# Moving the second mixer's preparation between the units of its weight stream, and rotating three tiles for normalised terms

## The reference

```
p = h @ w_in                                 # 1024 -> 2816 channels
ps, pc = p[:1792], p[1792:]                  # shifted part, convolution part
ps = ps + (token_shift(ps) - ps) * mu        # the frame before mixed in
r, k, v, xw, xa, xg = split(ps)              # 512, 512, 512, 64, 64, 128
decay = exp(-DECAY * sigmoid(w0 + tanh(xw) @ w_up))
a = sigmoid(a0 + xa @ a_up);   g = sigmoid(xg) @ g_up
kk = heads(k * k_k);  kk = kk * rsqrt(max(sum(kk*kk), 1e-12))   # 8 heads of 64
k = k * (1 + (a - 1) * k_a)
y = recurrence(r, decay, k, v, -kk, kk * a)  # 64 frames at a time
y = normalised per head * gn_w + gn_b + sum(r * k * r_k) * v
out_a = y * g
c = causal convolution of width 31 over glu(pc), one filter per channel
out_b = silu(layernorm(c))
return concatenate([out_a, out_b]) @ w_out
```

## Time and profile before

| what | value |
|---|---|
| median of three runs | 3702.67 us |
| the profiled execution's own time | 3696.74 us |
| its span in the profile | 3695.1 us, 45654 instructions |
| PE busy | 3479.5 us (94%) |
| DVE busy | 2001.3 us (54%) |
| ACT busy | 1122.0 us (30%) |
| mean granted TensorE clock | 0.976 of full |

### The profile page before, as it was taken

One profiled execution on the slowest core, in us unless ns is written; L12 is line 12 of the kernel. 1 busy time (PEld: TensorE's weight loads), 2 busy tenths in 40 slices (PEclk: granted clock), 3 DMA queues, 4 the chain that ended last, 5 costly groups with the idle time before them and its releaser, 6 DMA issues. The chain is left out here.

```text
span 3695.1 us, 45654 instructions
## 1 busy us (share of the span) xinstructions
PE 3479.5 (94%) x18472; PEld 2718.8 (74%) x18478; DVE 2001.3 (54%) x2662; ACT 1122.0 (30%) x1465; POOL 154.0 (4%) x128
## 2 busy tenths in 40 slices
PE   7999999999999999957799999999999989999998
PEld 6887776688878886837578886765788866568886
DVE  5667545522354334897753335696434348953334
ACT  2222335322232223232332223325322233452222
POOL 0000000000000000000000000330000012300000
PEclk8999999999999999979899999999999999999999
DMA  6554221122222222210012222210222221102221
GB/s 225 190 183 171 80 105 46 57 91 102 91 80 93 101 92 87 92 46 4 2 69 91 102 91 80 80 69 24 82 100 93 100 80 69 58 35 103 91 103 68
DMA packets 47213, 325.64 MB, mean 88 GB/s; under 512 B 5232, under 2 KB 5488, under 8 KB 8672
## 3 DMA queue, kind: packets, MB, share of 16 engines
q1 hardware_dynamic: 41792, 290.10, 22.0%
q0 software_dynamic: 5280, 33.52, 2.5%
HBM read 321.51 MB, written 2.10 MB: 88 GB/s over the span
## 5 line engine op out<-in xcount | busy, mean ns | idle before, releaser
L1991 PE MATMUL PS<-HH,WH 128*128 128x512 f32 x2264 | 895.2, 395 | 25.5 <-DVE HL L2392 18.9
L2374 DVE TENSOR_TENSOR WL<-RAW,WH 128x2048 fp32r<-128x2048 f32 x264 | 613.7, 2325 | 503.8 <-ACT WH L2227 498.2
L1992 PE MATMUL PS<-HL,WH 128*128 128x512 f32 x2264 | 884.8, 391 | 0.0
L1993 PE MATMUL PS<-HH,WL 128*128 128x512 f32 x2264 | 884.6, 391 | 0.0
L2227 ACT ACTIVATE WH<-RAW 128x2048 fp32r<-128x2048 f32 x264 | 503.1, 1906 | 330.2 <-PE PS L1993 322.1
L1991 PEld LDWEIGHTS PS<-HH,WH 128*128 128x128 f32 x2264 | 427.2, 189 | 140.6 <-issue 33.1
L1993 PEld LDWEIGHTS PS<-HH,WL 128*128 128x128 f32 x2264 | 427.0, 189 | 90.8
L1992 PEld LDWEIGHTS PS<-HL,WH 128*128 128x128 f32 x2264 | 427.3, 189 | 87.5 <-issue 1.2
L1991 PE MATMUL PS<-AH,WH 128*128 128x512 f32 x1056 | 412.3, 390 | 3.3 <-DVE A L2440 3.0
L1992 PE MATMUL PS<-AL,WH 128*128 128x512 f32 x1056 | 411.4, 390 | 0.0
L1993 PE MATMUL PS<-AH,WL 128*128 128x512 f32 x1056 | 411.3, 390 | 0.0
(11 more groups left out here) (395 smaller groups left out, 3668.2 us busy)
## 6 DMA issues: line engine op xcount, KB each, us to landing
RAW<-in_w SPq DMA_DIRECT2D x264, 1024.0 KB, 4.8
E<-in_ada POOLq DMA_DIRECT2D x28, 1024.0 KB, 5.0
E<-in_ada SPq DMA_DIRECT2D x4, 1024.0 KB, 11.8
G<-in_ada SPq DMA_DIRECT2D x4, 1024.0 KB, 19.3
X<-in_x SPq DMA_DIRECT2D x1, 2048.0 KB, 13.7
out_x<-A SPq DMA_DIRECT2D x8, 256.0 KB, 2.1
G<-in_cos POOLq DMA_DIRECT2D x4, 256.0 KB, 3.2
G<-in_sin POOLq DMA_DIRECT2D x4, 256.0 KB, 3.4
```

The lines of the kernel that those rows point to most:

```text
L1991: nc.tensor.matmul(out, wh, xh, start=start, stop=False)
L1992: nc.tensor.matmul(out, wh, xl, start=False, stop=False)
L1993: return nc.tensor.matmul(out, wl, xh, start=False, stop=stop)
L2374: nc.vector.tensor_tensor(WL[:, w % 2, :], RAW[:, w % 2, :], WH[:, w % 2, :].bitcast(F32), ALU.subtract).then_inc(w_lo, 1)
```

## The change

The order of the units becomes pc2, lora2, k2, r2, v2. The preparation is cut into pieces that stand between the units on all three engines. PE does the decay products behind unit 5, the rate products behind 6, the sum of squares of kk behind 7 (now to 32 rows a tile, all four tiles in one bank), the spreading of the root back to the heads behind 8, and the bonus behind 9. The projections use four banks in turn instead of eight, and the last unit its own two. The shift is made by ACT's copy with a scale (1 - mu) and one DVE operation that reads the bank. k_k, r_k and k_a are applied by ACT (r_k to the constant block matrix), and the bonus is copied out by ACT and multiplied by v later. The kk term takes the decay of the frame before out of the same sums, so that one exponential and one subtraction go. The last unit's shift, the multiplication of the bonus by v and the low half of the second w_out unit are done by DVE within the pairs. The taps run over up to three tiles in turn, so that a tap waits for the one before the last; 89 of the 124 stand in the stream and 35 in the pairs. The terms of normalised outputs take three tiles in turn and wait for the addition three tiles back.

```diff
-        "mix2": [("pc2", 4), ("r2", 2), ("k2", 2), ("v2", 2), ("lora2", 1)],
+        "mix2": [("pc2", 4), ("lora2", 1), ("k2", 2), ("r2", 2), ("v2", 2)],
...
+        B2, KK2 = A[:, 0:4, :], A[:, 4:8, :]
+        INV2, DEC2 = G[:, 16:20, :], A[:, 12:16, :]
+        TMP2 = [E[:, 15, :], E[:, 14, :], G[:, 20, :], G[:, 21, :]]
+        BV2 = [SG[:, 0, :], SG[:, 1, :], V[:], R0[:]]
+        RKB2 = A[:, 20, :]
+        BONUS_BANK, LAST_BANKS = (0, 1, 4, 5), (6, 7)
...
+        TAPS_IN = [9, 11, 11, 11, 9, 9, 14, 6, 2, 3, 4]
+        TAPS_LEVEL = [(2, 1, 2, 1, 1), (3, 2, 2, 1, 1), (3, 2, 2, 1, 1), (3, 2, 2, 1, 2)]
...
+        def chunk_of(q):
+            return (LO2, XG2)[q] if q < 2 else (K2, R2, V2)[(q - 2) // 4][:, (q - 2) % 4, :]
+        def mu_of(q):
+            return 12 + q if q < 2 else (4, 0, 8)[(q - 2) // 4] + (q - 2) % 4
+        def unit_banks(u):
+            return LAST_BANKS if u == U2 - 1 else (2 * (u % 2), 2 * (u % 2) + 1)
...
+            pool.dma_start(LEVELS[:, 0:7 * CH + 160], T["levels"]).then_inc(m2_loads, 16)
...
+                if 2 <= u < 6:
+                    pe.wait_ge(glu_done, u - 1)
+                elif u >= 6:
+                    pe.wait_ge(shifted, 2 * (u - 6) + 2)
+                h["project"](w + u, unit_banks(u), first=u == 0)
+                if u == 5:
+                    pe.wait_ge(m2_loads, 48)
+                    after("act", "low rank")
+                    for m in range(4):
+                        raise_(mm(PS[4 + m][:], LU2[0:64, m * P:(m + 1) * P], LO2[0:64, :], start=True, stop=True), "decay", m)
+                elif u == 6:
+                    for m in range(4):
+                        after("act", "sig d", m)
+                        raise_(mm(PS[4 + m][:], LU2[64:P, m * P:(m + 1) * P], LO2[64:P, :], start=True, stop=True), "rate", m)
+                elif u == 7:
+                    after("act", "kk sq")
+                    for m in range(4):
+                        last = mm(PS[4][32 * m:32 * m + 32, :], SEL2, TMP2[m], start=True, stop=True)
+                    raise_(last, "kk")
+                elif u == 8:
+                    after("dve", "kk root")
+                    for m in range(4):
+                        rows = slice(32 * m, 32 * m + 32)
+                        raise_(mm(PS[4 + m][:], SPREAD2[rows, :], R[rows, :], start=True, stop=True), "spread", m)
+                elif u == 9:
+                    after("act", "rkb")
+                    after("dve", "rk")
+                    after("dve", "kk")
+                    for m in range(4):
+                        raise_(mm(PS[BONUS_BANK[m]][:], RKB2[:, m * P:(m + 1) * P], TMP2[m], start=True, stop=True), "bonus", m)
...
+                if not a:
+                    after("dve", "scaled", m)
+                if m == 0:
+                    after("act", "bonus", 3)
...
+                pe.wait_ge(shifted, CHUNKS2)
...
+            def evacuate(u):
+                for c in range(2):
+                    q = 2 * (u - 4) + c
+                    ac(chunk_of(q), PS[unit_banks(u)[c]][:], ACT.Copy, scale=OM2[:, mu_of(q):mu_of(q) + 1]).then_inc(proj_evac, 1)
             for u in range(U2):
                 act.wait_ge(w_used, w + u + 1)
...
+                if u < U2 - 1:
+                    split(w + u + 2)
                 if u < 4:
                     if u >= 2:
                         act.wait_ge(glu_done, u - 1)
...
+                    ac(SG[:, u % 2, :], PS[unit_banks(u)[1]][:], ACT.Sigmoid).then_inc(gate_done, 1)
+                    continue
+                if u == 4:
+                    after("dve", "cols")
+                evacuate(u)
+                if u == 4:
+                    act.wait_ge(shifted, 2)
+                    ac(LO2[0:64, :], LO2[0:64, :], ACT.Tanh)
+                    raise_(ac(XG2, XG2, ACT.Sigmoid), "low rank")
+                elif u == 5:
+                    for m in range(4):
+                        after("pe", "decay", m)
+                        raise_(ac(INV2[:, m, :], PS[4 + m][:], ACT.Sigmoid, bias=col("w0", m)), "sig d", m, landed=False)
+                elif u == 6:
+                    for m in range(4):
+                        after("pe", "rate", m)
+                        raise_(ac(B2[:, m, :], PS[4 + m][:], ACT.Sigmoid, bias=col("a0", m)), "sig a", m, landed=False)
+                    for m in range(4):
+                        act.wait_ge(shifted, 3 + m)
+                        last = ac(KK2[:, m, :], K2[:, m, :], ACT.Copy, scale=col("k_k", m))
+                    raise_(last, "kk raw")
+                    after("dve", "sums", 3)
+                    for m in range(4):
+                        last = ac(TMP2[m], KK2[:, m, :], ACT.Square)
+                    raise_(last, "kk sq")
+                elif u == 7:
+                    after("pe", "kk")
+                    for m in range(4):
+                        last = ac(TMP2[m], B2[:, m, :], ACT.Identity, scale=col("k_a", m), bias=OM2[:, 14 + m:15 + m])
+                    raise_(last, "t2", landed=False)
+                    after("dve", "kk v")
+                    h["chain"](ac(R0[:], R[:], ACT.Ln))
+                    raise_(ac(R0[:], R0[:], ACT.Exp, scale=-0.5), "kk r0", landed=False)
+                    for m in range(4):
+                        last = ac(RKB2[:, m * P:(m + 1) * P], const("blocks"), ACT.Copy, scale=col("r_k", m))
+                    raise_(last, "rkb", landed=False)
+                    raise_(ac(INV2, DEC2, ACT.Exp, scale=DECAY), "inverse")
+                    raise_(ac(DEC2, DEC2, ACT.Exp, scale=-DECAY), "decays", landed=False)
+                elif u == 9:
+                    for m in range(4):
+                        after("pe", "bonus", m)
+                        raise_(ac(BV2[m], PS[BONUS_BANK[m]][:], ACT.Copy), "bonus", m, landed=False)
+            split(w + U2 + 1)
...
+            raise_(v.tensor_scalar(OM2[:, 0:14], col("mu", 0, 14), -1.0, 1.0, ALU.mult, ALU.add), "cols")
+            chain(v.tensor_scalar(OM2[:, 14:18], col("k_a", 0, 4), -1.0, 1.0, ALU.mult, ALU.add))
+            done, marked, latest = [0, 0, 0, 0], [None] * 4, [3]
...
+            def convolve(count, ready=4):
                 for _ in range(count):
+                    open_ = [m for m in range(min(ready, 3)) if done[m] < TAPS] or [m for m in (3,) if m < ready and done[m] < TAPS]
+                    open_ = [m for m in open_ if m != latest[0]] or open_
+                    if not open_:
+                        return
+                    m = min(open_, key=lambda x: done[x])
+                    if marked[m] is not None:
+                        chain.until(marked[m])
+                    marked[m] = chain.mark(tap(v, m, done[m]))
+                    done[m] += 1
+                    latest[0] = m
...
+            def shift(u):
+                for c in range(2):
+                    q = 2 * (u - 4) + c
+                    dest = chunk_of(q)
+                    dve.wait_ge(proj_evac, t("proj") + q + 1)
+                    v.scalar_tensor_tensor(dest[:, 1:], PS[unit_banks(u)[c]][:, 0:S - 1], col("mu", mu_of(q)), dest[:, 1:],
+                                           ALU.mult, ALU.add).then_inc(shifted, 1)
+            def sums():
+                for m in range(4):
+                    after("act", "sig d", m)
+                    raise_(v.tensor_tensor_scan(DEC2[:, m, :], SEG2, INV2[:, m, :], 0.0, ALU.mult, ALU.add), "sums", m, landed=False)
+            def key_root():
+                after("act", "kk r0")
+                chain(v.scalar_tensor_tensor(R[:], R[:], -0.5, R0[:], ALU.mult, ALU.mult))
+                chain(v.tensor_tensor(R[:], R[:], R0[:], ALU.mult))
+                raise_(v.scalar_tensor_tensor(R[:], R[:], 1.5, R0[:], ALU.add, ALU.mult), "kk root", landed=False)
+            def by_frame(x):
+                return x.rearrange("p (c s) -> p c s", s=CH)
+            def scaled(m):
+                v.tensor_tensor(R2[:, m, :], R2[:, m, :], DEC2[:, m, :], ALU.mult)
+                v.tensor_tensor(K2[:, m, :], K2[:, m, :], INV2[:, m, :], ALU.mult)
+                later = by_frame(KK2[:, m, :])[:, :, 1:]
+                v.tensor_tensor(later, later, by_frame(DEC2[:, m, :])[:, :, 0:CH - 1], ALU.mult)
+                raise_(v.tensor_tensor(B2[:, m, :], B2[:, m, :], INV2[:, m, :], ALU.mult), "scaled", m, landed=m == 3)
             for u in range(U2):
...
+                if u < U2 - 1:
+                    split(w + u + 2)
                 if u < 4:
                     dve.wait_ge(gate_done, u + 1)
...
+                    v.tensor_tensor(glu(u, TAPS - 1), PS[unit_banks(u)[0]][:], SG[:, u % 2, :], ALU.mult).then_inc(glu_done, 1)
                     dve.wait_ge(glu_done, u + 1)
+                elif u < U2 - 1:
+                    shift(u)
+                if u == 7:
+                    after("pe", "kk")
+                    raise_(v.tensor_scalar(R[:], PS[4][:], 1e-12, None, ALU.max), "kk v", landed=False)
+                    convolve(TAPS_IN[u])
```

(58 more changed lines are left out.)

137 lines of the change are left out of this document (13 added, 124 removed).

## The result

| kernel, in the same comparison | median | runs |
|---|---|---|
| before | 3703.29 us | 3702.51 to 3705.03 (4) |
| after | 3663.72 us | 3660.16 to 3664.57 (4) |

The ratio is 0.9894, with an interval of 0.9882 to 0.9906. The change makes the kernel 39.6 us faster, where 50.2 were forecast. The time lies in the range and 11 us above the forecast. The profiled execution after took 3663.09 us (span 3661.4 us, mean granted clock 0.979, PE busy 3485.5, DVE 1966.7 and ACT 1127.3 us).

What follows compares the result with a forecast made beforehand. DVE alone was taken to set 68 us behind a PE-set stream. Preparation 49.8 us earlier, less 4.6 in the pairs, plus 5.0 from terms, is 50.2: 3696.7 to 3646.5, plus 5.9 for the median, 3652.5 us; range 3642 to 3666.

Steps and rivals of the forecast that it cites:

- Its queue from unit 5 on: DVE's work in the stream from unit 5 to the first mask, laid out unit by unit, overfull from there.
- no drain: ACT's table loads: 1.28 us each without the skill's 1.38 us drain, by which the sum would be 3655.3.
- the queued split of ACT in unit 7: Unit 10's split, queued behind unit 7's ACT work, starts 4.6 us late; DVE waits 2.3 us.
- The price of the small products: Behind each of units 5 to 9, four small PE matmuls at 0.43 us each, 1.7 us together.
- Rival 1: Stall behind unit 8 lowers the clock (1.5 us), or ACT's unit 7 queue is longer: 3656.1; chance 0.15.
- The stall: Behind unit 8 PE waits 4.4 us for DVE's root, with unit 9 standing behind it.
- the 129.6 forecast: Second mixer's first split to first mask: the mask was forecast at 1621.0 instead of 1670.83, 49.8 us earlier.
- The pairs: 10.9 us of DVE work added in the pairs, partly hidden in idle time: 4.6 us later.
- about 7 us of idle PE: Sign expected in the profile: PE idle between the pairs' first products and the first step needing a mask.
- Rival 2: DVE becomes the pairs' bound and its added 10.9 us show in full: 3658.8; chance 0.12.
- The terms: Three tiles for terms: seven waits of 0.12 us saved in each of six sublayers, 5.0 us earlier.
- The base: Median of the runs lies 5.9 us above the profiled execution, so 3646.5 us became 3652.5.

Runs made afterwards that it cites:

- experiment 5: Kernel after, with decay, rate and bonus products made on only 128 of 512 frames (output not the reference's): 3661.15 us, ratio 0.9886.
- experiment 4: Kernel after, with the root of kk's norm ahead of the four multiplications of k2 in DVE's queue: 3660.64 us, ratio 0.9881.
- experiment 9: Kernel after, with three unread PE products in the stall behind unit 8, ahead of the spreading of the root: 3661.95 us, ratio 0.9882.
- experiment 3: Kernel after, with one idle DVE operation of 0.72 us added ahead of the first sublayer's terms: 3659.67 us, ratio 0.9882.
- experiment 6: Kernel after, with seven unread PE products between the pairs' first products and the first step that needs a mask: 3658.66 us, ratio 0.9881.
- experiment 7: Kernel after, without the pairs' seven added taps and four multiplications of the bonus by v (output not the reference's): 3659.52 us, ratio 0.9879.
- Experiment 1: Kernel before, with three tiles in turn for the terms and nothing else of the change: 3701.29 us, ratio 0.9993.
- experiment 2: Kernel after, with two tiles for the terms as before, so only the preparation is moved: 3665.35 us, ratio 0.9896.
- experiments 11 and 12: Kernel after with root first, seven unread products ahead of the masks, two taps ahead of query reading: 3658.87 us with three term tiles, 3657.24 with two.

## Why the prediction was right in kind and 11 us short

**What bounds, and the gain's kind: right.** DVE set the 68 us. Its queue from unit 5 on was laid out at 70.6 us and measured 70.3, with taps in turn at 0.67, scans, splits and table loads as in the rows of before (the logarithm 1.30 us after its load began, the second load 0.01 behind the logarithm's end; no drain). The two loads, the queued split of ACT in unit 7 and DVE's wait for it (2.3 forecast, 1.81 measured) came as told.

**The price of the small products: wrong, and with the stall's clock it makes the mask 4.5 us late.** The failed step is "PE 0.43 for one plain float matmul". The row counted records, and a float product is two of them: four take 3.7 to 3.9 us, not 1.7. With this the units behind the products last 14.8 us, ACT's splits come late and DVE waits 7.4 us instead of 2.5. With the products at 1.16 us a group 3.1 of the 4.5 us come back (experiment 5), and experiment 4 shows that 3 us could be had back by order with the products as they are.

**Rival 1 came true in its clock part.** The stall was 2.8 us, shorter than the 4.4 forecast since PE was later itself, yet the clock fell to 0.50, and that cost 2.9 us (experiment 9), where the rival had put 1.5 on it. It need not have: in experiment 3 the same stall left it at 1.00. Experiments 3, 4, 5 and 9 all end at a mask of 131.0 to 131.2, 1.4 behind the 129.6 forecast. In 3, 4 and 9 DVE has no wait left ahead of that unit's split, so its queue decides again. Without the half clock (3 and 9), without the stall (4) or with most of the products' price gone (5) the same 3 us come back: what was lost to them is not a sum, and none can be given a share of its own in these 3 us. The 1.4 that is left goes with DVE's waits for the earlier splits, 4.4 to 4.6 us in 3, 4 and 9 where 2.5 was forecast.

**The pairs: wrong, 4.7 us.** As far as the runs show, the failed step is one left out. The prediction itself forecast "about 7 us of idle PE" ahead of the first step that needs a mask, and it had the row in which 5.38 us of idleness left the clock at 0.50, but it charged the clock only to the stall in the stream, and only as a rival. The wait was 5.89 us and the clock was down for 9 us behind it. With that wait filled (experiment 6) the growth is 3.5 us, where 4.6 was forecast for DVE's work. But the half clock is not simply a term to be added where it lies: tile 0 grew by 3.2 us where 2.7 was forecast, and 4.4 of the 4.7 us too much stand in tile 2 and behind it (2.6 and 3.1 us, where 0.8 and 0.5 were forecast). They are gone in experiment 6 as well, and why stays open. Nor is the forecast of DVE's added work confirmed tile by tile; experiment 7, which takes out a part of it, finds 3.5 us where 3.1 was expected. Rival 2 (the 10.9 us in full) did not come.

**The terms: right in place, hardly seen in the time.** 4.3 us of the 5.0 stand in the trace. Experiment 1 lies 1.7 us below the kernel before and experiment 2 lies 1.6 above the kernel after (that one across two comparisons), experiments 11 and 12 lie 1.6 the other way. Whether the whole 4 us comes through in the median stays open: it is about the size of the clock's play.

**The base.** Taking the sum from the profiled execution's own time to the median by adding 5.9 was right here, and the comparison of the two profiled executions alone (−33.65) would have misled, as the one of before was lucky in the attention by 7.2 us. Here luck had a part: the 5.9 was the distance of one execution from the median, no row had shown what it came from, and without it the forecast would have been 17 us off.

## What to carry to other kernels

Before pricing a kind of matmul from a row, count how many records one call in the code leaves. Where an edit makes PE wait, look in the rows for waits of that length and the clock behind them, and put the half clock into the range or into the sum accordingly. Here waits of 2.78 us were followed by it in four profiled executions of five, and waits of 5.89 to 8.43 us ahead of the pairs in all eight. Then ask which engine sets the stretch behind: in tile 0, where DVE is the busier, 9 us at half clock were worth less than 1. Look also for the next wait to which a filling will only hand the loss. Compare stretches by their distance from a common milestone, and check the unchanged ones first: one of them held 7 us that had nothing to do with the change.

## What the runs showed of the hardware

In the first mixer's attention the clock fell to 0.50 in 13 of 14 profiled executions, for 20.5 us in ten of them (7.2 us of loss) and for 13.6 us in three (4.0 to 4.1 of loss), with PE busy all but 0.06 us before it (6.00 of 6.00 us at 590 to 596 and 5.94 of 6.00 at 596 to 602 in the kernel after, and as much in the one execution in which it stayed at 1.00). No run tells what decides it, nor why a wait of 2.78 us was followed by half clock in the kernel after and in experiments 2, 6 and 7, and not in experiment 3. In tile 1 of the pairs of the kernel after it fell too, and with PE's wait in tile 0 filled it did not. Seven unread float products (6.28 us of PE) went with pairs that were 5.8 us shorter, of which 0.8 lay in the tile behind them.
